# Square root and reciprocal in place of logarithm and exponential in the head norm of the first mixer

## The reference

```python
y = rwkv7_recurrence(rh, heads(decay), kh, vh, -kk, kk * ah.astype(jnp.float32))
mean = jnp.mean(y, axis=-1, keepdims=True)
var = jnp.mean(jnp.square(y - mean), axis=-1, keepdims=True)
y = ((y - mean) * lax.rsqrt(var + RW_LN_EPS)).reshape(bsz, t_len, RW_WIDTH)
y = (y * ln_g + ln_b).astype(h.dtype)
bonus = jnp.sum(rh * kh * r_k, axis=-1, keepdims=True) * vh
o_rw = (y + bonus.reshape(bsz, t_len, RW_WIDTH)) * g
```

## Time and profile before

| what | value |
|---|---|
| median of 3 runs | 2608.23 us (2606.58 to 2608.91) |
| the profiled execution | 2613.38 us, its span 2611.6 us |
| TensorE busy in the span | 2277.7 us (87%) |
| VectorE, ScalarE busy | 1211.5 us (46%), 926.6 us (35%) |
| mean granted TensorE clock | 0.942 |
| last chain: TensorE, DMA, VectorE, ScalarE | 60%, 26%, 7%, 6% |
| the four norms of the change | from 151.6 to 187.7 us |

### The profile page before, as it was taken

One profiled execution on the slowest core, in us unless ns is written; L12 is line 12 of the kernel. 1 busy time (PEld: TensorE's weight loads), 2 busy tenths in 40 slices (PEclk: granted clock), 3 DMA queues, 4 the chain that ended last, 5 costly groups with the idle time before them and its releaser, 6 DMA issues.

```text
span 2611.6 us, 38789 instructions
## 1 busy us (share of the span) xinstructions
PE 2277.7 (87%) x17182; PEld 1728.0 (66%) x17182; DVE 1211.5 (46%) x1731; ACT 926.6 (35%) x1331; POOL 1.4 (0%) x6
## 2 busy tenths in 40 slices
PE   8998666666989766676999999999999999999998
PEld 7773122122755211122899999989989999888997
DVE  4543212121872111111555588665456547866554
ACT  4141000001142000000555577554345546865543
POOL 0000000000000000000000000000000000000000
PEclk9998888888989888878999999999999999999999
DMA  6419999999258999999744443445444435334442
GB/s 283 163 59 377 428 428 428 428 428 426 93 207 342 427 428 428 428 428 427 282 145 179 166 149 142 162 177 194 168 172 162 166 135 189 139 144 170 172 183 105
DMA packets 48062, 662.99 MB, mean 254 GB/s; under 512 B 5328, under 2 KB 5584, under 8 KB 7824
## 3 DMA queue, kind: packets, MB, share of 16 engines
q1 hardware_dynamic: 47664, 659.17, 62.7%
q0 software_dynamic: 224, 1.26, 0.1%
HBM read 659.36 MB, written 1.05 MB: 253 GB/s over the span
## 4 chain that ended last, share of the span: by engine, by line
PE 60%; DMA 26%; DVE 7%; ACT 6%; issue 1%; SPq 0%; DVEq 0%; ACTq 0%
DMA ring<-w_dram 26%; PE ps L2457 8%; PE ps L2459 8%; PE ps L2458 8%; PE ps L1917 3%; PE ps L878 3%; PE ps L1342 2%; PE ps L2717 2%; PE ps L2718 2%; PE ps L2719 2%; PE ps L910 2%; PE ps L3323 1%; PE ps L3321 1%; PE ps L3322 1%; ACT r L2434 1%
## 5 line engine op out<-in xcount | busy, mean ns | idle before, releaser
L2445 DVE TENSOR_TENSOR r<-ring,r 128x1024 fp32r<-128x1024 f32 (+1 forms) x392 | 505.6, 1301 | 343.4 <-ACT r L2434 342.8
L2457 PE MATMUL ps<-r 128*128 128x256 f32 x2112 | 608.4, 288 | 8.3 <-DVE r L2529 5.5
L2458 PE MATMUL ps<-r 128*128 128x256 f32 x2112 | 599.3, 284 | 0.0
L2459 PE MATMUL ps<-r 128*128 128x256 f32 x2112 | 599.2, 284 | 0.0
L2434 ACT ACTIVATE r<-ring 128x1024 fp32r<-128x1024 f32 (+1 forms) x392 | 430.6, 1116 | 271.6 <-PE ps L2459 135.3
L878 PE MATMUL ps<-ring 128*32 128x512 f32 x1952 | 299.4, 746 | 185.7 <-DMA ring<-w_dram 185.6
L2457 PEld LDWEIGHTS ps<-r 128*128 128x128 f32 x2112 | 406.5, 192 | 14.8 <-issue 7.4
L2458 PEld LDWEIGHTS ps<-r 128*128 128x128 f32 x2112 | 406.8, 193 | 0.2
L2459 PEld LDWEIGHTS ps<-r 128*128 128x128 f32 x2112 | 406.6, 193 | 0.0
L878 PEld LDWEIGHTS ps<-ring 128*32 128x32 f32 x1952 | 61.7, 123 | 408.7 <-DMA ring<-w_dram 204.5
L1124 DVE TENSOR_TENSOR arena<-ps,arena 128x512 f32<-128x512 f32 x16 | 11.1, 692 | 443.0 <-PE ps L878 443.0
(11 more groups left out here) (446 smaller groups left out, 3155.8 us busy)
## 6 DMA issues: line engine op xcount, KB each, us to landing
ring<-w_dram SPq DMA_DIRECT2D x302, 2048.0 KB, 22.9
arena<-w_dram SPq DMA_DIRECT2D x6, 2048.0 KB, 14.4
ring<-w_dram SPq DMA_DIRECT2D x4, 1024.0 KB, 4.8
arena<-w_dram SPq DMA_DIRECT2D x1, 1536.0 KB, 7.3
x<-x_dram SPq DMA_DIRECT2D x2, 512.0 KB, 3.8
ring<-w_dram SPq DMA_DIRECT2D x2, 512.0 KB, 12.8
out_dram<-x SPq DMA_DIRECT2D x4, 256.0 KB, 2.0
cst<-w_dram SPq DMA_DIRECT2D x1, 973.0 KB, 24.3
```

The lines of the kernel that those rows point to most:

```text
L2445: v.tensor_tensor(lo, w, hi.bitcast(F32), SUB).then_inc(*S.up(f"lo {s}", *(["free " + name] if last else [])))
L2457: pe.matmul(out, hi[:, k, :], K.HH[:, k, :], start=k == 0, stop=False)
L2458: pe.matmul(out, hi[:, k, :], K.HL[:, k, :], start=False, stop=False)
L2459: r = pe.matmul(out, lo[:, k, :], K.HH[:, k, :], start=False, stop=k == 7)
```

## The change

The logarithm becomes a square root with the same input, scale and bias, the exponential with its wait goes, and VectorE takes the reciprocal of the 128x256 slice in place before it multiplies with it.

```diff
@@ the chunks of ScalarE @@
         a.wait_ge(*K.after(nm + "var"))
-        a.activation(b.LD[:, hp, :], K.banks[nm + "var"][:, 0:256], ACT.Ln, bias=K.par("epsln"),
-                     scale=1.0 / 64).then_inc(*S.up(nm + "var read"))
-        a.wait_ge(*S.now())
-        a.activation(b.LD[:, hp, :], b.LD[:, hp, :], ACT.Exp, scale=-0.5).then_inc(*S.up(nm + "rs"))
+        a.activation(b.LD[:, hp, :], K.banks[nm + "var"][:, 0:256], ACT.Sqrt, bias=K.par("epsln"),
+                     scale=1.0 / 64).then_inc(*S.up(nm + "var read", nm + "root"))
         yield
@@ the chunks of VectorE @@
         yield
-        wait(nm + "rs")
+        wait(nm + "root")
+        v.reciprocal(b.LD[:, hp, :], b.LD[:, hp, :]).then_inc(*S.up())
         own()
         tt(R, R, b.LD[:, hp, :], MUL)
         own()
```

## The result

| | before | changed |
|---|---|---|
| median | 2608.03 us (12 runs, 2604.86 to 2610.88) | 2612.39 us (12 runs, 2606.72 to 2614.76) |
| ratio, 95% interval | | 1.0016 (1.0008 to 1.0023) |
| profiled execution, its span | 2613.38, 2611.6 us | 2614.20, 2612.4 us |

The changed kernel is slower by 4.4 us, with an interval of 2.1 to 6.0 us. The forecast was +1.8 us and 2610.0, in a range of 2606.0 to 2613.5. A second set of 11 runs of the changed kernel against 33 of the one before gave 1.0010 (1.0001 to 1.0019).

What follows compares the result with a forecast made beforehand. It took TensorE's progress through the mixer to set the start of a transfer-bound expert-weight stage. Norm steps of 1.24 + 0.42 + 0.06 + 0.04, say 1.8 us, on 2608.23 gave 2610.0 us, range 2606.0 to 2613.5.

Steps and rivals of the forecast that it cites:

- A: Rival on VectorE's norms: the reciprocal is as cheap as a product, 0.42 us, total 2606.8 us; chance 0.08.
- B: Rival on VectorE's norms: the reciprocal takes eight product passes per column, 2.3 us, total 2612.2 us; chance 0.10.
- C: Rival: TensorE's longer pause at pair 0 brings another clock fall, 3.4 us more, total 2613.4 us; chance 0.10.
- The price of the reciprocal: VectorE, each of the four norms: a reciprocal of 256 columns takes 1.75 us, between 0.42 and 2.3 us.
- the lower of my two slopes: VectorE reciprocal's growth per column: 6.1 ns (from 1 and 16 columns), against 6.7 ns (from 2 and 16).
- The order argument: VectorE works in order, so each reciprocal delays the next pair's step S2, for which TensorE waits; 1.76 us over four norms.
- full clock from 150 to 190 us: Through the mixer, TensorE's granted clock was to stay full, as before the change.
- Rival D: The weight stream sets the time anyway and swallows the mixer's shift; total 2608.2 us, chance 0.05.
- each microsecond there moves everything behind it by one: TensorE's progress to the mixer's end sets the start of the transfer-bound expert stage, so delays pass on in full.
- ScalarE's 11.9 us: ScalarE's saving: eight table loads, 10.3 us, and four exponentials, 1.7 us, go; waits cost only where TensorE waits too.

Runs made afterwards that it cites:

- experiment 7: Kernel before plus two unneeded VectorE reciprocals (125 and 87 columns) at the norm of pair 0; median 2609.93 us, ratio 1.0007.
- experiment 9: Changed kernel plus four unneeded TensorE products during its wait for the S2 sum of pair 1; 2610.11 us, ratio 1.0008.
- experiment 3: Changed kernel with pair 0 kept on logarithm and exponential, pairs 1 to 3 changed; median 2607.97 us, ratio 1.0002.
- experiment 12: Changed kernel with the norm of pair 0 one round later and that of pair 3 in halves of 128 tokens; 2606.44 us, ratio 1.0000.
- experiment 1: Changed kernel with the reciprocal replaced by a multiplication by one; total 4808.92 us (not comparable, expert work changed), mixer 33.94 us.
- experiments 8 and 4: 8: kernel before plus reciprocals of 125 and 28 columns at pair 0, 2603.00 us once; 4: changed kernel, norms 0 to 2 one round later, 2606.86 us.

## Why the prediction was right, and where it was not

**The side and the class.** I forecast no change that a measurement could tell, on the slower side. The measured 0.16% lies inside the range and below 0.2%, but its interval begins at 0.08% and that of the second set at 0.01%, so it is a small loss and not nothing. That the time fell into the range owes something to luck: the range was made for other cases (A, B and the start of C), and in the mixer a term that I had put at nothing, the clock, cost as much as all that I had added up.

**The price of the reciprocal** came out as reckoned: 1.748 us against 1.75, carried from rows of 1, 2 and 16 columns. With 948 ns for 128 columns the slope is (1748 - 948)/128 = 6.25 ns a column, so the lower of my two slopes was the better. Rival B, eight passes a column, is refuted, and so is A. The iterated divide with a repeat count of 8 in the Trainium skill (VectorE: DVE Perf Modes, First, the fixed hardware budget) cannot be read as eight product passes a column: at 1.05 ns a pass the slope is six.

**Where the time went.** The order argument held at each pair: 1.24 forecast and 1.14 measured at pair 0; 0.42 and 0.28 at pair 1; 0.06 and 0.00 to 0.06 at pair 2; 0.04 and 0.05 at pair 3. The small excess comes from overlaps: the reciprocal starts 0.08 us before the instruction ahead of it has ended (156.24 against 155.90 + 0.42), and at pair 1 the S2 sum starts 0.08 us before the products end (174.39 against 173.59 + 0.88), where I had let each start after. The sum is 1.46 us, not 1.76.

**The step that failed** is the one that held all else still, "full clock from 150 to 190 us". Rival C, to which I gave 0.10, is what happened. Its mechanism was right: experiment 7 produces the low clock with the pause alone, experiment 9 removes it by filling the pause, and behind a pause of 1.64 us it did not come. Its price was too high: 1.55 us in the mixer instead of 3.4, because I took the fall after the mixer for a measure, and this one is half as long (3.4 us at the half level instead of 6.8). Even for the fall after the mixer 3.4 us was too much: the hand-over took only 2.55 us less in the two traces without that fall. With it the sum is 1.46 + 1.55 = 3.0 us, which the mixer shows in both traces and which the interval of 2.1 to 6.0 us holds. My argument against it, that TensorE is busy right up to the pause, was no protection.

**Rival D** is refuted for the part that can be seen: in every trace the hand-over is the same 47.15 us or shorter by a difference in the clock, whatever the mixer took, and the first weight wait moved with the mixer. But "each microsecond there moves everything behind it by one" is not shown further on. The changed kernel keeps its distance up to about 400 us and not to 812 us, and the next 570 us scatter by 8 us between the traces. The clearest pair is the kernel before and that of experiment 3: they are 0.16 us apart at a weight wait at 594 us (594.33 and 594.17) and 5.7 us apart at 812 us, and from 700 to 800 us the granted clock is 0.93 in the one and 0.97 in the other. Which of the later stages' clock and transfers gives and takes this time stays open. Thus the 3.0 us of the mixer can't be followed to the end of the program. The medians of the changed kernel, 4.4 and 1.6 us over before in the two sets, and of experiment 7, 3.0 over, agree with it but do not prove it; that of experiment 9, 3.1 over with a mixer only 1.5 longer, shows how loosely they follow the mixer.

**The prize that was none.** ScalarE's 11.9 us are gone as forecast, and VectorE's waits for the exponential with them, and no time came of it. At pair 3, where the exponential and its load were on the chain, the reciprocal took their place: 1.75 us and its handovers for 1.76, a pause 0.05 us longer.

## What to carry to other kernels

When work moves from one engine to another, price what it stands in front of in the new engine's queue, not only its own length. Here the same 1.75 us cost almost nothing at pairs 2 and 3, where VectorE had waited about as long for the exponential. It cost 1.14 us at pair 0, where that wait had been only 0.55 us and TensorE stood waiting for the sum behind.

A pause of TensorE can cost more than itself: at pair 0 one of 2.02 us brought on a stretch at the half clock, one of 1.64 us did not, and a few unneeded products in the wait took it away. A reciprocal over a whole tile on VectorE takes some four times as long as a product of the same tile (1748 against 424 ns), and its time grows with the columns. The norm has only one value for each head and token, but whether a form with fewer columns would pay was not tried.

## What the runs showed of the hardware

- VectorE's reciprocal in float32: 253 ns for 16 columns, 948 for 128, 1748 for 256, that is 6.25 ns a column against 1.05 for a product.
- TensorE's granted clock at the same place in the program: full behind pauses of 0.57, 0.88, 1.23, 1.28 and 1.64 us, at the half level (1.2 of 2.4 GHz) for 3.4 us behind 2.02 us in three of three traces (two kernels), full again when the same wait was filled with products. The other lengths have one trace each, except 0.88 with two. This is no rule for pauses elsewhere: the low clock after the mixer came behind a pause at pair 3 of 1.50 or 1.55 us, but also behind one of 0.49 us (experiment 12) and with none (experiment 1), and in two traces with 1.49 and 1.55 us there (experiments 8 and 4) it did not come. So the bound between 1.64 and 2.02 us is not sure either: a second execution with 1.64 us is missing.
- The low clock after the mixer is not tied to a kernel. The hand-over took 47.15 us in nine traces with 6.8 us at the half level, 44.60 in two with full clock throughout, and 45.48, 45.48 and 46.17 in three with 3.4 us at the half level. What decides it stays open. It is worth up to 2.55 us, nearly as much as the whole loss in the mixer.
